# An encoder layer with 16 experts: weights laid out by unit, one prompt gate/up group, and the tail's first loads issued ahead of the stage border

## The reference, cut to what matters

```python
def expert_choice_moe(h, w_router, w_gate, w_up, w_down):      # per group; 16 experts, D_EXPERT = 512
    cap = CAPACITY_FACTOR * N // N_EXPERTS                     # 128 tokens of sample, 64 of prompt
    ...
    gates, idx = lax.top_k(aff.T, cap)
    xe = hf[idx]
    a = jnp.einsum('ecd,edf->ecf', xe, w_gate)
    u = jnp.einsum('ecd,edf->ecf', xe, w_up)
    ye = jnp.einsum('ecf,efd->ecd', jax.nn.silu(a) * u, w_down)
    ye = gates[..., None].astype(ye.dtype) * ye
    out = jnp.zeros_like(hf).at[idx].add(ye)

# tail
    gate = jax.nn.sigmoid(rmsnorm(x, g_ple[i]) @ w_ple_gate[i])
    x = x + gate * (p[i] @ w_ple_proj[i])
return rmsnorm(x, g_final)
```

## Time and profile before

| | us |
|---|---|
| median of 3 runs (lowest to highest) | 1625.5 (1622.51 to 1626.88) |
| the profiled execution | 1623.36 |
| its span, first to last instruction | 1621.5 |
| PE busy | 1447.0 (89%), mean granted clock 0.947 |
| DVE, ACT, POOL busy | 932.7, 721.8, 182.2 |
| experts' stage | 936.8 to 1452.6 |
| tail | 1452.6 to 1621.5 |

### The profile page before, as it was taken

The page is one execution under the profiler, slowest core; times in us unless marked ns, Lnnn a source line. Parts: engine busy times, 40 slices in busy tenths (PEclk is TensorE's granted clock), DMA queues, the critical chain, the costliest instruction groups (busy, mean ns, idle before and its releaser), DMA issues. The chain is left out here.

```text
span 1621.5 us, 21520 instructions
## 1 busy us (share of the span) xinstructions
PE 1447.0 (89%) x7320; PEld 1016.2 (63%) x7320; DVE 932.7 (58%) x1324; ACT 721.8 (45%) x1157; POOL 182.2 (11%) x255
## 2 busy tenths in 40 slices
PE   5999997599999969869998969999999999948997
PEld 4777775365565535458887746666666666627885
DVE  5444443377677748723347856677676676643553
ACT  4333433376666747722221544444444444423332
POOL 1111111000000000010000111112112121021110
PEclk9999998699999979989998979999999999978999
DMA  8533322713111054064432756878878788753331
GB/s 257 94 111 110 110 97 85 252 64 114 70 63 55 20 190 156 29 208 156 140 123 87 262 169 220 263 252 270 256 261 267 254 262 265 245 164 126 126 135 65
DMA packets 118847, 261.53 MB, mean 161 GB/s; under 512 B 7648, under 2 KB 37472, under 8 KB 115720
## 3 DMA queue, kind: packets, MB, share of 16 engines
q1 hardware_dynamic: 110592, 233.55, 41.2%
q0 software_dynamic: 7168, 25.17, 6.7%
q10 hardware_dynamic: 1032, 2.10, 1.1%
HBM read 194.20 MB, written 66.58 MB: 161 GB/s over the span
## 5 line engine op out<-in xcount | busy, mean ns | idle before, releaser
L1742 DVE TENSOR_TENSOR moe_w_lo<-ring,moe_w_hi 128x2048 fp32r<-128x2048 f32 x96 | 220.3, 2296 | 163.5 <-ACT moe_w_hi L1681 163.4
L1681 ACT ACTIVATE moe_w_hi<-ring 128x2048 fp32r<-128x2048 f32 x96 | 183.7, 1914 | 204.0 <-PE moe_p_g L1864 82.2
L1413 PE MATMUL mix_p_big<-kept_out_w,mix_m_hi 128*128 128x512 f32 x384 | 126.4, 411 | 4.6 <-DVE mix_m_lo L1288 2.4
L510 PE MATMUL proj_p_out<-proj_w_hi,proj_h_hi 128*128 128x512 f32 x264 | 110.8, 420 | 9.5 <-DVE proj_q_hl L408 9.5
L1872 PE MATMUL moe_p_gu<-ring,moe_xT_r 128*64 128x512 f32 x512 | 116.9, 598 | 0.0
L510 PE MATMUL proj_p_out<-proj_w_lo,proj_h_hi 128*128 128x512 f32 x264 | 105.0, 398 | 0.0
L510 PE MATMUL proj_p_out<-proj_w_hi,proj_h_lo 128*128 128x512 f32 x264 | 104.9, 397 | 0.0
L962 DVE TENSOR_REDUCE sample_ntop<-sample_p_s 128x1 f32<-128x1024 f32 x64 | 78.2, 1222 | 37.4 <-PE sample_p_s L784 36.7
L798 PEld LDWEIGHTS sample_p_t<-sample_ident_r,sample_probs_r 128*128 128x128 f32 x688 | 73.1, 142 | 23.2 <-ACT sample_probs L900 6.6
L1413 PEld LDWEIGHTS mix_p_big<-kept_out_w,mix_m_hi 128*128 128x128 f32 x384 | 73.1, 196 | 21.4 <-issue 2.6
L798 PE MATMUL sample_p_t<-sample_ident_r,sample_probs_r 128*128 128x128 f32 x688 | 80.1, 246 | 5.0 <-ACT sample_probs L900 2.5
(11 more groups left out here) (298 smaller groups left out, 3122.4 us busy)
## 6 DMA issues: line engine op xcount, KB each, us to landing
ring<-in_w_gate SPq DMA_DIRECT2D x32, 1024.0 KB, 5.6
ring<-in_w_up SPq DMA_DIRECT2D x32, 1024.0 KB, 7.6
ring<-in_w_down SPq DMA_DIRECT2D x32, 1024.0 KB, 7.2
qT_d<-proj_qT SPq DMA_DIRECT2D x12, 1024.0 KB, 3.9
sample_q<-qT_d SPq DMA_DIRECT2D x8, 1024.0 KB, 5.3
proj_x<-in_x SPq DMA_DIRECT2D x12, 512.0 KB, 4.3
proj_w_raw<-in_w_in SPq DMA_DIRECT2D x8, 768.0 KB, 5.6
kT_d<-proj_kT SPq DMA_DIRECT2D x12, 512.0 KB, 3.6
```

Source lines behind the costliest of these rows:

```text
L510: last = pe.matmul(p_out[:, cols], h[:, s, k, :], w[:, k, cols], start=(k == 0 and n == 0), stop=(k == KC - 1 and n == 2))
L1413: mm = pe.matmul(p_out[:, cols], m[:, s, k, :], ww[:, k, cols], start=(k == 0 and n == 0), stop=(k == KC - 1 and n == 2))
L1681: act.activation(w_hi[:, at % SPLIT], raw[:, at % RAW], ACT.Copy).then_inc(hi_made, 1)
L1742: dve.tensor_tensor(w_lo[:, at % SPLIT], raw[:, at % RAW], w_hi[:, at % SPLIT].bitcast(F32), ALU.subtract).then_inc(lo_made, 1)
```

## The change

- On the host the weights are laid out by unit: `w_gate` and `w_up` as (16, 2, 128, 2048), `w_down` likewise by column halves, so that a unit is 1 MB in one piece and a partition's part one row of 8 KB. `expert_unit` follows.
- The prompt's gate/up matmuls of both halves stand together behind the four sample units. The first pair's `pair_done` comes after its 16 matmuls there.
- A new class `TailInputs` holds the tail's x tiles (laid over the ring's first two slots), `g_ple`, and their semaphores. SP of the experts' stage loads `g_ple`, waits for the first two splits of the tail's weights and for the last sample scatter, and issues x tiles 0 to 3. POOL's two waits at the end are gone.
- In the tail SP starts with the two tiles of `ple_d` and then `g_final`; ahead of x tile 8 it waits for the prompt scatters. DVE waits for `g_ple` ahead of the first norm and for `g_final` ahead of the first final norm.

```diff
-    w = w[row] if isinstance(row, int) else w[bass.ds(row, 1)].rearrange("a r c -> (a r) c")
-    w = w.rearrange("(k p) c -> p k c", p=P)
-    return w[:, j // 2 * FC:(j // 2 + 1) * FC, :] if j < 4 else w[:, :, (j - 4) * BANK:(j - 3) * BANK]
+    part = j // 2 if j < 4 else j - 4
+    w = w[row, part] if isinstance(row, int) else w[bass.ds(row, 1), part].rearrange("a p n -> (a p) n")
+    return w.rearrange("p (k c) -> p k c", c=BANK)
...
+class TailInputs:
+    X = 4
+    def __init__(self, kept, ring):
+        self.x = ring[:, 0:self.X * D].rearrange("p (s d) -> p s d", d=D)
+        self.g = kept.sb("g_ple", [P, D])
...
+    def load(self, sp, acc_d, t):
+        sp.dma_start(self.x[:, t % self.X, :], acc_d[t * P:(t + 1) * P, :]).then_inc(self.x_landed[t % self.X], 16)
...
+            following.load_gain(sp, g_ple)
+            sp.wait_ge(pg_lo_made, 2)
+            sp.wait_ge(ys_added, 16 * E)
+            for t in range(following.X):
+                following.load(sp, acc_d, t)
...
-            pool.wait_ge(ys_added, 16 * E)
-            pool.wait_ge(yr_added, 16 * E)
...
-                if half == 0 and later(e, 1):
-                    pe.wait_ge(mul_made, e * 2)
-                prompt(p_gu, at - 1, xT_r, half * FC, half == 0, half == 1)
+                if half == 1:
+                    if later(e, 1):
+                        pe.wait_ge(mul_made, e * 2)
+                    prompt(p_gu, at - 3, xT_r, 0, True, False)
+                    prompt(p_gu, at - 1, xT_r, FC, False, True)
...
+                sp.wait_ge(x3_made, t - X + 1)
+                if t == SAMPLE_TILES:
+                    sp.wait_ge(inputs.prompt_added, 16 * EXPERTS)
+                inputs.load(sp, acc_d, t)
...
-            load(0)
-            sp.dma_start(g_all[:], g_ple.partition_broadcast(P)).then_inc(g_landed, 16)
-            sp.dma_start(gf_all[:], g_final.partition_broadcast(P)).then_inc(g_landed, 16)
-            load(1)
             load_e(0)
             load_e(1)
-            for t in range(2, X):
-                load(t)
+            sp.dma_start(gf_all[:], g_final.partition_broadcast(P)).then_inc(g_landed, 16)
...
+                if t == 0:
+                    dve.wait_ge(g_landed, 16)
...
-            dve.wait_ge(g_landed, 32)
+            dve.wait_ge(inputs.g_landed, 16)
```

More of the change, by code:

```diff
@@ L1506, in _, with load_gain, experts @@
             pe.transpose(p_slots[:, ROWS:2 * ROWS], at_f[:], ident[0:ROWS, 0:ROWS]).then_inc(turned, 1)
-def experts(nc, h_d, acc_d, w_gate, w_up, w_down, gates, slots, ring, ring_r, raw_landed, w_pg, pg_hi, pg_lo):
+class TailInputs:
[3 more added lines that the diff above has]
+        self.g = kept.sb("g_ple", [P, D])
+        self.x_landed, self.g_landed = kept.sems("tail_x_landed", self.X), kept.sem("g_ple_landed")
+        self.sample_added, self.prompt_added = kept.sem("sample_added"), kept.sem("prompt_added")
+    def load_gain(self, sp, g_ple):
+        sp.dma_start(self.g[:], g_ple.partition_broadcast(P)).then_inc(self.g_landed, 16)
+    def load(self, sp, acc_d, t):
+        sp.dma_start(self.x[:, t % self.X, :], acc_d[t * P:(t + 1) * P, :]).then_inc(self.x_landed[t % self.X], 16)
+def experts(nc, h_d, acc_d, w_gate, w_up, w_down, gates, slots, ring, ring_r, raw_landed, w_pg, pg_hi, pg_lo,
+            g_ple, following):
     S, R = 2 * T_SAMPLE // EXPERTS, 2 * T_PROMPT // EXPERTS
@@ L1548, in experts @@
         weighed = sem("weighed")
-        ys_added, yr_added = sem("ys_added"), sem("yr_added")
+        ys_added, yr_added = following.sample_added, following.prompt_added
+        pg_lo_made = sem("pg_lo_made")
         block = ctx.enter_context(nc.Block())
@@ L1734, in split_pg @@
                 dve.tensor_tensor(pg_lo[:, 2 * m:2 * m + 2, :], pg_raw(m), pg_hi[:, 2 * m:2 * m + 2, :].bitcast(F32),
-                                  ALU.subtract)
+                                  ALU.subtract).then_inc(pg_lo_made, 1)
             def split(e, t):
@@ L1918, in _, with embed_out @@
             over_steps(pe, step)
-def embed_out(nc, acc_d, ple_d, w_hi, w_lo, g_ple, g_final, y):
-    X = 4
+def embed_out(nc, acc_d, ple_d, w_hi, w_lo, inputs, g_final, y):
+    X = inputs.X
     with ExitStack() as ctx:
@@ L1926, in embed_out @@
         ident, ident_r = sb("ident", [P, P]), sb("ident_r", [P, P], F32R)
-        g_all, gf_all = sb("g_all", [P, D]), sb("gf_all", [P, D])
+        g_all, gf_all = inputs.g, sb("gf_all", [P, D])
         nhalf, eps = sb("nhalf", [P, 1]), sb("eps", [P, 1])
-        x_sb, e_sb = sb("x", [P, X, D]), sb("e", [P, 2, D])
+        x_sb, e_sb = inputs.x, sb("e", [P, 2, D])
         sq = sb("sq", [P, 2, D], mybir.dt.bfloat16)
@@ L1936, in embed_out @@
         cleared, ident_ready, consts, g_landed = sem("cleared"), sem("ident_ready"), sem("consts"), sem("g_landed")
-        x_landed, e_landed = sems("x_landed", X), sems("e_landed", 2)
+        x_landed, e_landed = inputs.x_landed, sems("e_landed", 2)
         IN, OUT = 0, 1
@@ L1949, in load @@
             def load(t):
-                if t >= X:
-                    sp.wait_ge(x3_made, t - X + 1)
-                sp.dma_start(x_sb[:, t % X, :], acc_d[t * P:(t + 1) * P, :]).then_inc(x_landed[t % X], 16)
+                sp.wait_ge(x3_made, t - X + 1)
+                if t == SAMPLE_TILES:
+                    sp.wait_ge(inputs.prompt_added, 16 * EXPERTS)
+                inputs.load(sp, acc_d, t)
             def load_e(t):
@@ L2161, in encoder_layer @@
         pg_hi, pg_lo = kept.sb("pg_hi", [P, KC, D], F32R), kept.sb("pg_lo", [P, KC, D], F32R)
-        experts(nc, h_d, acc_d, *experts_w, gates, slots, ring, ring_r, raw_landed, i["w_ple_gate"], pg_hi, pg_lo)
-        embed_out(nc, acc_d, ple_d, pg_hi, pg_lo, i["g_ple"], i["g_final"], y)
+        following = TailInputs(kept, ring)
+        experts(nc, h_d, acc_d, *experts_w, gates, slots, ring, ring_r, raw_landed, i["w_ple_gate"], pg_hi, pg_lo,
+                i["g_ple"], following)
+        embed_out(nc, acc_d, ple_d, pg_hi, pg_lo, following, i["g_final"], y)
 def t5_buckets():
@@ L2211 @@
         arrays[name] = i[name][0]
+    for name in ("w_gate", "w_up"):
+        w = arrays[name].reshape(EXPERTS, 2, FC, P, D_EXPERT)
+        arrays[name] = np.ascontiguousarray(w.transpose(0, 1, 3, 2, 4)).reshape(EXPERTS, 2, P, UNIT)
+    w = arrays["w_down"].reshape(EXPERTS, FC, P, 2, BANK)
+    arrays["w_down"] = np.ascontiguousarray(w.transpose(0, 3, 2, 1, 4)).reshape(EXPERTS, 2, P, UNIT)
     nc = _bacc.Bacc("TRN2", target_bir_lowering=False, num_devices=1)
```

## The result

| | before | after |
|---|---|---|
| median of 6 runs, us | 1626.19 (1622.51 to 1627.12) | 1634.21 (1630.96 to 1635.99) |
| ratio, 95% interval | | 1.0053 (1.0037 to 1.0068) |
| profiled execution, its span, us | 1623.36, 1621.5 | 1635.38, 1633.6 |

The changed kernel is 8.0 us slower: outside the 0.3% that a measurement can tell, and inside the predicted range, but with less than half of the forecast's +18.5. It stands at rival B (the waits, without clock falls: +8.5, 1634) and not at the forecast's 1643. The profiled executions are 12.0 us apart, since before's lies 2.8 under its median and after's 1.2 over its own.

A forecast was written before the change was run, and what follows sets the result against it. PE's own stream was taken to bound the experts' stage. Waits +12.6, expert 0 +3.8, expert 15 +0.9, clock falls +10 and tail -8.8 gave +18.5 us on the 1625.5 median, about 1643; range 1618 to 1660.

The forecast's parts named there:

- rival B: PE waits in 14 experts but its clock never falls: +8.5 us, 1634 (1630 to 1636); chance 0.22.
- The bound: Experts' stage: PE's own stream sets the time, so a faster transfer by itself gives nothing there.
- The saving: PE's gate/up matmuls: merging the two prompt groups saves 0.52 us an expert, 8 us over 16.
- The moved refill, the load and the chain: Next expert's gate load, 4.8 us, then 5.8 through ACT and DVE: PE waits 1.4, expert ends 0.9 later, 14 times.
- C: Moved load lands within 3.4 us, so experts gain and the kernel is faster: -14 us, 1611; chance 0.11.
- D: Moved load lands at about break-even: experts +0, expert 0 +2.9, tail -8.8, 1620; chance 0.07.
- E: Moved load takes 4.4 us and the shorter wait moves no clock: +2.5 us, 1628; chance 0.10.
- Expert 0: First expert, no slack: the later refill puts PE at 975.1 instead of 971.32, +3.8 us (2.9 to 4.3).
- Expert 15: Last expert: DVE's later low split delays the hidden copy that down(15) waits for, +0.9 us (0 to 1.5).
- The clock falls: Half-speed PE stretches behind the new waits, 1.7 us each, in 5 of 14 experts and expert 0: +10 us (0 to 25).
- The 5.3 within the tail: Tail's start to PE's first product: x loads and gains already issued, so the product comes 5.3 us earlier.
- The 3.5 at the drain: End of experts: GpSimd's 5.29 us drain starts once its last scatter is issued, so the tail starts 3.5 us earlier.

The follow-up runs named there:

- the cure: Changed kernel with the split of the next expert's first gate unit put behind silu, multiply and the x halves on ACT and DVE: 1608.56 us, ratio 0.9909.
- ACT's order alone: Changed kernel with the split of the next expert's first gate unit put behind silu_prompt and x_high on ACT only, DVE unchanged: 1634.65 us, ratio 1.0057.

## Why the prediction was right, and where it was not

**The bound.** PE's stream set the period, and what is faster beside it gave nothing (the layout alone: 0). Right.

**The saving**, 0.52 an expert: 0.43 where it comes through. The joint between the two prompt halves gives less than was put in: from first to last start the merged group takes 6.50 us (7.09 less 0.59) and the two groups of before 3.06 each, so the joint costs 0.38 and not 0.204. That is 0.17 too little; the joint of the sample units gives some of it back. Small, right in kind.

**The moved refill, the load and the chain.** The load of 4.8 us and the chain of 5.8 came out to 0.1. The wait was put at 1.4 and measured 1.07 to 1.36; the net of 0.9 an expert is 0.88 in experts 2 to 14 of the profile, the one fall left out. The page "DMA: Bandwidth & Descriptors" of the Trainium skill, section "Anatomy of one DMA", gave an estimate of 4.4, by its figures for GpSimd's path; this load of SP's took 4.8 in the trace, 0.4 more, as the nearest row had said. The moved loads of experts 1 to 14 took 4.65 to 4.95. Rivals C, D and E needed a load of 4.4 or less and fall.

**Expert 0**, +3.8: 3.2 net. **Expert 15**, +0.9: PE idles 2.60 instead of 1.79 at down(15), and its last matmul is 0.5 later. Both within their bounds.

**The clock falls** are the term that was mis-sized: 6 x 1.7 = 10 us forecast. Measured were one fall of 1.7 in experts 1 to 14 and, at the border of experts 0 and 1, a longer stretch at half speed, of which 4.75 us instead of 2.8 fell on expert 1's matmuls: some 0.8 us (its +1.65 less the 0.88 of the others), an estimate. Together 2.5 instead of 10. The step "I take it for 5 of 14" leaned on a row with a fall at 1.79 of idle and one without at 1.41 and put the new wait between them. The runs place it better: 8 of 14 at 1.8 to 2.05 us of wait, 1 of 14 at 1.07 to 1.36, none of 14 at 0 in the cure. This is rival B, whose sum of +8.5 is what the medians show. The group alone in the old layout is what the forecast's mechanism looks like when it does act: +40 us.

**The tail.** The 5.3 within the tail came to 5.2. The 3.5 at the drain failed: the step "its closing drain of 5.29 us starts there" took a fixed length from the end of the issue, but the drain ends 2.7 us behind the last landing, and that landing came 7.8 us after the issue instead of 6.7, with the first of the four x loads issued 2.8 us behind it. Of the 2.8 us that the waits are worth 1.7 were left. The prediction had named this case as its lower bound ("0 if the drain ends only with the landings"); it is half true, since the drain does end by the landing, but closer behind it than before. The x loads themselves were in time, as forecast.

**The sum.** The experts without falls, +17.3 (12.6 + 3.8 + 0.9), came to 16.0 in the profile, 18.5 with the clock's 2.5; the tail gave -6.9 and its clock -1.3, which was not forecast. That makes +10.3, and with the 1.8 us ahead of the first expert, where the change does nothing, the profiles' 12. The medians' +8.0 (6.0 to 11.1 by the ratio's interval) can't tell this from rival B's 8.5. The errors went both ways: the falls 7.5 us and the experts' rest 1.3 too many, the drain 1.8 too good, the tail's clock 1.3 not seen. That the result lies so close to rival B is in part luck. A slip of adding stands in the forecast too: 1625.5 and 18.5 are 1644, not 1643.

**Missed altogether:** that the wait stood in the order of two queues and not in the load. The prediction listed what stands behind the landing, correctly, and did not ask whether it has to. That order was worth 23 to 26 us, three times what the whole change cost.

## What to carry to other kernels

When a load is moved later, list what stands behind its landing in each in-order queue; if work that does not need the data stands there, move that work ahead in every one of those queues, since a single queue left as it was (ACT or DVE alone) loses the same time at another line. A merge that saves 0.4 us on the bound engine is worth taking only together with that. And a faster transfer is worth its time exactly where it is waited for: nothing in before and in the cured kernel, but with the group merged and the wait in place some 24 us (1.0243 against the 1.0095 that the group costs in the new layout). Of these 24 the load itself makes up 9 (14 x 0.65) and seven more clock falls 12, by the profiles.

## What the runs showed of the hardware

GpSimd's drain behind indirect DMAs: 5.29 us when it starts behind an awaited landing, so that it ends 5.5 us behind that landing (in all five kernels with the waits). Without the waits it ends 2.7 us behind the last landing (in all eight kernels without them, which land 6.5 to 8.2 us after the issue). Why these two lengths is not settled.

GpSimd's last scatter landed 6.5 to 6.7 us after its issue in nine kernels, and 7.0 to 8.2 in the four in which the first of four 512 KB loads was issued 2.7 to 3.5 us behind it. The moved 1 MB load took 4.65 to 4.95 us with 8 KB rows (after) and 5.4 to 5.6 with 2 KB rows (the group alone).

The granted clock behind the waits ahead of `turn_x_prompt`: 0.50 after 8 of 14 waits of 1.8 to 2.05 us, after 1 of 14 of 1.07 to 1.36 (the changed kernel) and after 2 of 14 of 1.12 to 1.67 (ACT's order alone). In the last the falls came behind waits of 1.30 and 1.33, while it stayed at 1.00 behind 1.54 and 1.67. So longer waits go with more falls from kernel to kernel, but within a kernel the length does not tell which wait is followed by one; what does is open.
